# Hybrid streaming encoder step: the sample stage's loads all issued by the sync engine, the output weights split at that stage's tail, and the projection's last stores awaited inside it

## The chip, the core and the metric

The kernel runs on one core of a Trainium2 chip. The metric is the device time of one execution in microseconds (us); lower is better. The engines are PE (matrix products), DVE (vector), ACT (scalar activations), POOL and SP. SP computes nothing here, it issues DMAs. ACT can issue DMAs too, and while it does it computes nothing.

## What is computed

One layer of an encoder runs for one prompt (2048 tokens) and eight short sample streams (8 x 16 tokens = one tile of 128 rows), which share all weights:

```python
h = _rmsnorm(x, g_mix) * (1 + sc1) + sh1
qa, ka, va, qb, kb, vb, ob, ib, fb, zc, xbc, dtc, ud, vd = _split_cols(h @ w_in, IN_SIZES)
y_a = _band_attention(qa, ka, va, k_hist, v_hist, a_rel_bias)      # samples: 512 cached keys each
hb, new_bc, new_bn, new_bm = _mlstm(qb, kb, vb, igate, logf, b_c, b_n, b_m)
yc, new_ssm = _ssd(xs, dt, a, bm, cm, c_ssm)
mix = jnp.concatenate([y_a, y_b, y_c, y_d], axis=-1) @ w_out
x = x + gt1 * mix
x = x + gt2 * ((silu(causal_dwconv3(h2 @ w_gate)) * (h2 @ w_up)) @ w_down)
```

## The kernel before

Five stages follow each other, each a block in which every engine has its own written-out instruction order: `modulation` (0 to about 127 us of the profiled execution), `projections` (to about 834), `sample_stage` (to about 967), `mixers` (to about 1527), `feed_forward` (to the end). Between two stages all engines meet at a barrier (`Semaphores.give_back`, which also clears the stage's semaphores). No engine starts a stage before SP has passed the last waits of the stage before.

- **End of `projections`.** SP issues the last stores: the convolution rows to the scratch tensor `xc`, then `p_c_conv`, three DMAs of 768 single 4-byte elements each (L437). Then it waits for every store of the stage (L440 to L447), and the barrier follows.
- **`sample_stage`.** SP issues the loads of the cached keys and values (`k_in`, `v_in`, 8 + 8 DMAs of 512 KB) and of the SSM states (`ssm`, 8 of 128 KB). ACT, ahead of its first activation, issues everything else: gate parameters (`row_par`, `m0`), `qt`, `tok`, `xc`, `qa`, `k_new`, `v_new`, eight bias pieces, the mLSTM states `cst` (4 DMAs of 64-element rows and 4 of single elements, `state_b_n`), `gc` and `skip` (L1496 to L1518). PE then turns keys, computes scores for two streams at a time, multiplies with the old states (`old_c`, L1371, which waits for all of `cst`; `old_h`), and so on to `new_h` (L1427). DVE first places `qa` in `q_blk` (L1707), then builds the gate rows (L1710 to L1742). At the end SP stores `y`, the attention rows `ya` and the new states, `s_c_ssm` last (L1298).
- **`mixers`.** It multiplies with `w_out` in a split form: `w_hi` is the weight rounded to the PE's fast format (ACT, L2329), `w_lo` the remainder (DVE, L2590), and each product is three matmuls (L2148 to L2150). The eight slices of `w_out` are loaded through two buffers at the head of this stage; slice n+2 is loaded once `w_lo` of slice n is made. ACT's order is: slices 0 and 1, `decays(0)` (L2325), slices 2 to 7, and then the loop over the tiles, whose first step keeps `xs_b` (L2340). DVE's order is: wait for `params` (band, `gc`, four `skip_col` loads), two memsets of `band`, `skip`, `add_columns(0)` (L2454), the eight `w_lo`, then the loop. PE begins with `turn_xs` (L2053), which waits for `skip`. The first loop step multiplies the sample tile with `w_out`.

The two orders on ACT and DVE in `mixers`:

```python
for n in range(KD):                                   # ACT, L2327
    act.wait_ge(s_w[n % 2], 16 * (n // 2 + 1))
    a.activation(w_hi[:, KO[n], :], w_raw[n % 2], ACT.Copy).then_inc(E["w_hi"], 1)
    if n == 1:
        decays(0)
for n in range(KD):                                   # DVE, L2588
    dve.wait_ge(E["w_hi"], n + 1)
    v.tensor_tensor(w_lo[:, KO[n], :], w_raw[n % 2], w_hi[:, KO[n], :], ALU.subtract).then_inc(E["w_lo"], 1)
```

Of the kernel before, what the change touches and what calls it, by code (L numbers as in the profile page):

```python
# [11 lines left out]
P = 128  # L12
# [213 lines left out]
def projections(nc, sem, A, O, S, c, keep, par, w_hi, w_lo):  # L226
# [17 lines left out]
    with ExitStack() as ctx:  # L244
# [87 lines left out]
        def _(sp):  # L332
# [108 lines left out]
            for n in range(2):  # L441
                sp.wait_ge(s_xst[n], 16 * sum(len(tokens(m // KX)) for m in range(KX * NGR) if m % 2 == n))
# [4 lines left out]
            sp.wait_ge(s_copy, 16 * N_COPIES)  # L447
# [186 lines left out]
        def _(dve):  # L634
# [381 lines left out]

C_FLOOR, C_WB, C_WC, C_A, C_NCS = range(5)


def modulation(nc, sem, A, S, c, const_program, keep, par, w_hi, w_lo):  # L1020

    with ExitStack() as ctx:
# [25 lines left out]
        s_gout, s_par = sem("gates_stored"), sem("params_loaded")  # L1048
# [34 lines left out]
        def _(act):  # L1083
# [13 lines left out]
            act.wait_ge(s_par, 16 * len(par["loads"](A)))  # L1097

# [101 lines left out]
def sample_stage(nc, sem, A, O, S, c, par):  # L1200
# [4 lines left out]
    with ExitStack() as ctx:  # L1205
        sb, ps = new_pools(nc, ctx, "s_")
        W1 = DH + 1
        k_in, v_in = sb("k_in", [P, NB, NPAST, GW]), sb("v_in", [P, NB, NPAST, GW])
        k_t = sb("k_t", [P, 2, NB, HIST])
# [9 lines left out]
        row_par = sb("row_par", [H, 6])  # L1219
        cst, m0 = sb("cst", [P, 2, NB, W1]), sb("m0", [H, NB])  # L1220
# [19 lines left out]
        gc, skip = sb("gc", [P, GW]), sb("skip", [P, H])  # L1240
# [7 lines left out]
        names = """rows_loaded att_in bias_loaded mix_in par_in cst_loaded ssm_loaded  # L1248
# [15 lines left out]
        def _(sp):  # L1264
# [6 lines left out]
            for j in range(NG):  # L1271
                load_kv(2 * j)
                load_kv(2 * j + 1)
                if j == 0:
                    for b in range(NB):
                        sp.dma_start(ssm[half(b), b // 2], A["state_c_ssm"][0, b].rearrange("h p n -> p h n")
                                     ).then_inc(E["ssm_loaded"], 16)
                load_v(2 * j)
                load_v(2 * j + 1)
            sp.wait_ge(E["ready"], 1)  # L1280
# [212 lines left out]
        def _(act):  # L1493
            a = nc.scalar
            step = Steps(act, E["act"])
            for n, name in enumerate(("b_i_bias", "b_f_bias", "c_dt_bias", "c_a_log")):  # L1496
                act.dma_start(row_par[:, n:n + 1], A[name].rearrange("a h -> h a"), allow_slow_non_contiguous=True
                              ).then_inc(E["rows_loaded"], 16)
            act.dma_start(m0[:], A["state_b_m"][0].rearrange("b h -> h b"), allow_slow_non_contiguous=True
                          ).then_inc(E["rows_loaded"], 16)  # L1500
            act.dma_start(qt[:], S["qb"][:, :, SEQ:SEQ + P]).then_inc(E["mix_in"], 16)
            act.dma_start(tok[:], S["tok"][SEQ:SEQ + P, :]).then_inc(E["mix_in"], 16)
            act.dma_start(xc[:], S["xc"][:, :, SEQ:SEQ + P]).then_inc(E["mix_in"], 16)
            act.dma_start(qa[:], S["qa"][:, :, SEQ:SEQ + P]).then_inc(E["att_in"], 16)
# [32 lines left out]
            act.wait_ge(E["rows_loaded"], 80)  # L1537
# [47 lines left out]
            keep_probs(3)  # L1585

        @block.gpsimd
        def _(pool):
# [11 lines left out]
            pool.wait_ge(E["par_in"], 32)  # L1600
# [52 lines left out]
        def _(dve):  # L1653
# [183 lines left out]
            extract(3)  # L1837
            for h in range(H):
                add_h(h)


def mixers(nc, sem, A, O, S, c, keep, par):

# [5 lines left out]
    with ExitStack() as ctx:  # L1849
# [61 lines left out]
        def _(sp):  # L1911
# [82 lines left out]
            for n in range(2, KD):  # L1994
                load_w(n)
# [1301 lines left out]
```

## Time and profile before

| | |
|---|---|
| median of 3 runs | 3177.63 us (3173.46 to 3180.89) |
| the profiled execution | 3168.1 us, of which the span of instructions is 3166.4 us |
| PE busy in the span | 2846.8 us (90%) |
| DVE, ACT, POOL busy | 1297.1, 982.1, 245.0 us |
| HBM traffic | 285.75 MB read, 70.10 MB written |

The profiled execution is 9.5 us shorter than the median. Its span differs from its own time by 1.7 us. "Busy" is the time in which an engine executes an instruction; issuing a DMA is not counted as busy, although the engine can do nothing else meanwhile.

### The profile page before, as it was taken

What the parts mean: (1) busy time and instruction counts of PE and PEld (TensorE: products, weight loads), DVE (VectorE), ACT (ScalarE), POOL (GpSimd) and SP (SyncE); (2) the same over time, 40 slices, a digit from 0 to 9 for tenths busy, and PEclk for the clock granted to TensorE, in tenths of its full rate; (3) what the DMA queues carried; (4) which work ended last, traced back from release to release, by engine and by line L of the source; (5) the groups of instructions that cost most, each with busy time, mean ns of one, the idle gap of its engine ahead of it and who ended that gap; (6) DMA issues with size and microseconds to landing.
All of it is one profiled execution on the core that took longest, in us unless ns stands there. A gap on an engine that the chain in (4) does not pass through costs nothing.

```text
span 3166.4 us, 41936 instructions
## 1 busy us (share of the span) xinstructions
PE 2846.8 (90%) x16292; PEld 2548.5 (80%) x16292; DVE 1297.1 (41%) x2483; ACT 982.1 (31%) x1682; POOL 245.0 (8%) x413
## 2 busy tenths in 40 slices
PE   4499999999272999999599999999999999999987
PEld 1288888999252788887599998789999878999975
DVE  2333334342142554554233334544433454544444
ACT  1133334332131444444222223332222333222333
POOL 0000000000021432332000000000000000000000
PEclk8699999999685999999699999999999999999998
DMA  9622324211517444342522224433222443322344
GB/s 296 213 72 93 109 71 153 89 67 70 166 15 201 152 140 126 125 129 71 138 61 66 60 66 141 158 109 104 64 62 66 135 156 113 114 73 74 99 130 145
DMA packets 342266, 355.48 MB, mean 112 GB/s; under 512 B 44423, under 2 KB 283659, under 8 KB 341684
## 3 DMA queue, kind: packets, MB, share of 16 engines
q1 hardware_dynamic: 326738, 349.02, 35.4%
q10 hardware_dynamic: 15396, 4.66, 0.8%
q8 instruction: 88, 1.44, 0.2%
q14 instruction: 44, 0.36, 0.0%
HBM read 285.75 MB, written 70.10 MB: 112 GB/s over the span
## 4 chain that ended last, share of the span: by engine, by line
PE 46%; DVE 2%; DMA 2%; SPq 1%; issue 1%; ACT 0%; POOL 0%; DVEq 0%; ACTq 0%
PE acc_ps L2873 14%; PE acc_ps L2829 11%; PE acc_ps L2830 11%; PE acc_ps L2831 11%; DMA w_raw<-in_f_w_down 1%; DMA xr<-scratch_x 0%; DVE y L3121 0%; SPq L2773 0%; DVE w_lo L3095 0%; DMA out_y_prompt<-y 0%; ACT w_hi L2968 0%; DVE xr L3115 0%; DMA ffn_gate_in<-scratch_ffn_gate 0%; DVE prod L3109 0%; DVE w_lo L3038 0%
## 5 line engine op out<-in xcount | busy, mean ns | idle before, releaser
L2829 PE MATMUL acc_ps<-h_hi,w_hi 128*128 128x384 f32 (+1 forms) x2112 | 690.3, 327 | 6.3 <-DVE w_lo L3038 6.1
L2830 PE MATMUL acc_ps<-h_lo,w_hi 128*128 128x384 f32 (+1 forms) x2112 | 689.5, 326 | 0.0
L2831 PE MATMUL acc_ps<-h_hi,w_lo 128*128 128x384 f32 (+1 forms) x2112 | 689.5, 326 | 0.0
L3038 DVE TENSOR_TENSOR w_lo<-w_raw,w_hi 128x1024 fp32r<-128x1024 f32 x242 | 296.5, 1225 | 662.7 <-ACT w_hi L2926 652.9
L2926 ACT ACTIVATE w_hi<-w_raw 128x1024 fp32r<-128x1024 f32 x242 | 256.6, 1060 | 800.5 <-PE acc_ps L2831 524.0
L2829 PEld LDWEIGHTS acc_ps<-h_hi,w_hi 128*128 128x128 f32 x2112 | 397.9, 188 | 7.8 <-DVE w_lo L3038 6.5
L2830 PEld LDWEIGHTS acc_ps<-h_lo,w_hi 128*128 128x128 f32 x2112 | 397.9, 188 | 0.1
L2831 PEld LDWEIGHTS acc_ps<-h_hi,w_lo 128*128 128x128 f32 x2112 | 397.8, 188 | 0.0
L2873 PE MATMUL acc_ps<-w_hi,mid_hi 128*128 128x512 f32 x748 | 236.1, 397 | 30.3 <-DVE mid_lo L3099 15.8
L2873 PE MATMUL acc_ps<-w_hi,mid_lo 128*128 128x512 f32 x748 | 233.2, 393 | 0.0
L2873 PE MATMUL acc_ps<-w_lo,mid_hi 128*128 128x512 f32 x748 | 233.0, 393 | 0.0
L881 PE MATMUL p_unit<-w_in_hi,p_ht_hi 128*128 128x512 f32 (+1 forms) x544 | 203.2, 373 | 2.1 <-ACT p_m L490 2.1
L881 PE MATMUL p_unit<-w_in_hi,p_ht_lo 128*128 128x512 f32 (+1 forms) x544 | 200.9, 369 | 0.0
L881 PE MATMUL p_unit<-w_in_lo,p_ht_hi 128*128 128x512 f32 (+1 forms) x544 | 200.3, 368 | 0.0
L2873 PEld LDWEIGHTS acc_ps<-w_hi,mid_hi 128*128 128x128 f32 x748 | 139.5, 190 | 69.5 <-DVE mid_lo L3099 22.4
L940 PE MATMUL p_unit<-p_ht_hi,w_in_hi 128*128 128x384 f32 (+1 forms) x576 | 190.2, 330 | 2.8 <-DVE p_ht_lo L707 1.6
L941 PE MATMUL p_unit<-p_ht_lo,w_in_hi 128*128 128x384 f32 (+1 forms) x576 | 189.2, 329 | 0.0
L942 PE MATMUL p_unit<-p_ht_hi,w_in_lo 128*128 128x384 f32 (+1 forms) x576 | 188.6, 327 | 0.0
L2873 PEld LDWEIGHTS acc_ps<-w_lo,mid_hi 128*128 128x128 f32 x748 | 142.0, 190 | 30.3
L2873 PEld LDWEIGHTS acc_ps<-w_hi,mid_lo 128*128 128x128 f32 x748 | 142.0, 190 | 30.1
L3024 POOL TENSOR_SCALAR ff_mean<-ff_ss 128x1 f32<-128x1 f32 x17 | 8.7, 510 | 1629.1 <-ACT prod L2973 1629.1
L3073 DVE TENSOR_TENSOR mid<-gate_on,acc_ps 128x384 f32 (+3 forms) x132 | 64.3, 529 | 162.6 <-PE acc_ps L2831 162.6
(490 smaller groups left out, 4155.7 us busy)
## 6 DMA issues: line engine op xcount, KB each, us to landing
w_raw<-in_f_w_down SPq DMA_DIRECT2D x122, 512.0 KB, 3.5
w_raw<-in_f_w_gate SPq DMA_DIRECT2D x66, 512.0 KB, 3.9
w_raw<-in_f_w_up SPq DMA_DIRECT2D x66, 512.0 KB, 3.9
w_ada<-in_w_ada SPq DMA_DIRECT2D x12, 2048.0 KB
m_bc<-scratch_bc SPq DMA_DIRECT2D x16, 768.0 KB, 5.1
scratch_tok<-p_m SPq DMA_DIRECT2D x17, 640.0 KB, 2.9
m_tok<-scratch_tok SPq DMA_DIRECT2D x16, 640.0 KB, 4.8
scratch_ht<-p_m SPq DMA_DIRECT2D x17, 512.0 KB, 3.3
```

What stands on the lines that cost most here:

```text
L881: last = t.matmul(dst, a[j][:, k, :], b[:, k, at:at + w], start=(k == 0 and a is th_hi and b is w_hi), stop=(k == KD - 1 and a is th_lo))
L940: t.matmul(dst, w_hi[:, k, cols], hi, start=(k == 0), stop=False)
L941: t.matmul(dst, w_hi[:, k, cols], lo, start=False, stop=False)
L942: last = t.matmul(dst, w_lo[:, k, cols], hi, start=False, stop=(k == KD - 1))
L2829: t.matmul(dst, hi, h2_hi[:, k, cols], start=(k == 0), stop=False)
L2830: t.matmul(dst, hi, h2_lo[:, k, cols], start=False, stop=False)
L2831: last = t.matmul(dst, lo, h2_hi[:, k, cols], start=False, stop=(k == KD - 1))
L2873: last = t.matmul(acc[:, pair, half, :], lhs[j][:, cols], rhs[j][:, half * 512:(half + 1) * 512], start=begin, stop=(stop and lhs is m_lo))
L2926: a_.activation(w_hi[j][:], raw[j][:], ACT.Copy).then_inc(s_hi[j], 1)
L3024: nc.gpsimd.tensor_scalar(mean[:, j:j + 1], ss[:, j:j + 1], 1.0 / D, EPS, ALU.mult, ALU.add).then_inc(s_mean, 1)
L3038: v.tensor_tensor(w_lo[j][:], raw[j][:], w_hi[j][:], ALU.subtract).then_inc(s_lo[j], 1)
L3073: last = v.tensor_tensor(at_f(mid, f)[:, at:at + w], gate_on[:, at:at + w], u_ps[:, b, 0:w], ALU.mult)
```

## The change

- **Projection's last waits.** SP no longer waits at the end of `projections` for the `xc` stores and for five copies (`p_c_conv` among them). Their three semaphores survive the barrier, and the waits (`p_stored`) stand in `sample_stage`: on POOL before it writes `v1`, on DVE before `nums`, on SP before the store of `y`.
- **Parameters.** `row_par`, `m0`, `gc`, `skip` and `skip_col` become persistent (`par[...]`) and are loaded in `modulation` by 11 DMAs from ACT, behind the bias rows. The loads of the same data in `sample_stage` (7) and `mixers` (5) are gone.
- **Sample loads.** ACT issues none. SP issues all: `tok`, `xc`, `qt`, keys 0 and 1, `qa`, `k_new`, `v_new`, bias, `ssm`, values 0 and 1, `cst`, and then the other keys and values.
- **Output weights.** Once all keys are turned, SP loads the eight slices of `w_out` into the keys' buffer (now called `w_raw`). Behind the last attention copy ACT makes `w_hi` (in the memory of the turned keys), behind the last state DVE makes `w_lo` (in place of `w_raw`). `mixers` loads and splits nothing; there `skip` and `add_columns(0)` stand ahead of the wait for `band`.
- In `projections`, `m_row` and `diag` become views of the tile `vn`.

```diff
@@ projections, SP
-            for n in range(2):
-                sp.wait_ge(s_xst[n], 16 * sum(len(tokens(m // KX)) for m in range(KX * NGR) if m % 2 == n))
-            sp.wait_ge(s_copy, 16 * N_COPIES)
+        def stored(engine):
+            for n in range(2):
+                engine.wait_ge(s_xst[n], 16 * sum(len(tokens(m // KX)) for m in range(KX * NGR) if m % 2 == n))
+            engine.wait_ge(s_copy, 16 * N_COPIES)
@@ modulation, ACT
             rel_store(act)
+            for dst, at in par["more"](A):
+                act.dma_start(dst, at, allow_slow_non_contiguous=True).then_inc(s_more, 16)
@@ sample_stage, SP
-            for j in range(NG):
+            sp.dma_start(tok[:], S["tok"][SEQ:SEQ + P, :]).then_inc(E["mix_in"], 16)
+            sp.dma_start(xc[:], S["xc"][:, :, SEQ:SEQ + P]).then_inc(E["mix_in"], 16)
+            sp.dma_start(qt[:], S["qb"][:, :, SEQ:SEQ + P]).then_inc(E["mix_in"], 16)
+            load_kv(0)
+            load_kv(1)
...
+            for j in range(1, NG):
                 load_kv(2 * j)
                 load_kv(2 * j + 1)
...
                 load_v(2 * j)
                 load_v(2 * j + 1)
+            sp.wait_ge(E["k_turned"], 2 * NB)
+            w_view = A["w_out"][0].rearrange("(k p) n -> k p n", p=P)
+            for k in range(KD):
+                sp.dma_start(w_raw[:, k, :], w_view[k]).then_inc(E["w_loaded"], 16)
+            p_stored(sp)
@@ sample_stage, ACT
-            for n, name in enumerate(("b_i_bias", "b_f_bias", "c_dt_bias", "c_a_log")):
-                act.dma_start(row_par[:, n:n + 1], A[name].rearrange("a h -> h a"), allow_slow_non_contiguous=True
-                              ).then_inc(E["rows_loaded"], 16)
...
-            act.dma_start(skip[:], A["c_d_skip"][0].partition_broadcast(P)).then_inc(E["par_in"], 16)
...
             keep_probs(3)
+            act.wait_ge(E["w_loaded"], 16 * KD)
+            act.wait_ge(E["scores"], NG)
+            for k in range(KD):
+                a.activation(w_hi[:, k, :], w_raw[:, k, :], ACT.Copy).then_inc(E["w_high"], 1)
@@ sample_stage, POOL
+            pool.wait_ge(E["mix_in"], 48)
+            p_stored(pool)
             step(g.memset(v1[:, :, DH:W1], 1.0))
-            pool.wait_ge(E["mix_in"], 48)
@@ sample_stage, DVE
             dve.wait_ge(E["qc_kept"], 1)
+            p_stored(dve)
             step(v.tensor_tensor(nums[:], qc[:], spread(col[:, R_INTER, :], 2, W1), ALU.mult))
...
+            for k in range(KD):
+                dve.wait_ge(E["w_high"], k + 1)
+                v.tensor_tensor(w_lo[:, k, :], w_raw[:, k, :], w_hi[:, k, :], ALU.subtract).then_inc(E["w_low"], 1)
@@ mixers, ACT
-            for n in range(KD):
-                act.wait_ge(s_w[n % 2], 16 * (n // 2 + 1))
-                a.activation(w_hi[:, KO[n], :], w_raw[n % 2], ACT.Copy).then_inc(E["w_hi"], 1)
-                if n == 1:
-                    decays(0)
+            decays(0)
@@ mixers, DVE
-            dve.wait_ge(E["params"], 16 * N_PARAMS)
...
             for g in range(2):
                 v.tensor_scalar(skip[:, g, :], c["ident"][:], skip_col[:, g:g + 1], None, ALU.mult).then_inc(E["skip_made"], 1)
             add_columns(0)
-            for n in range(KD):
-                dve.wait_ge(E["w_hi"], n + 1)
-                v.tensor_tensor(w_lo[:, KO[n], :], w_raw[n % 2], w_hi[:, KO[n], :], ALU.subtract).then_inc(E["w_lo"], 1)
+            dve.wait_ge(E["band_loaded"], 16)
@@ the kernel
-                projections(nc, sem, A, O, S, c, keep, par, w_hi, w_lo)
+                p_stored = projections(nc, sem, A, O, S, c, keep, par, w_hi, w_lo)
+            sem.give_back(but=("p_xc_stored0", "p_xc_stored1", "p_copies"))
```

On ACT, at the start of the sample stage, this stood before (the last of its loads and its first activations; `s_` is the stage's prefix of tile names, `s_m` the PSUM tile):

```order
L1510 DMA s_bias_in<-scratch_rel 16x528 x8
L1513 DMA s_cst<-in_state_b_c 64x8x64
L1515 DMA s_cst<-in_state_b_n 64x8x1
L1513 DMA s_cst<-in_state_b_c 64x8x64
L1515 DMA s_cst<-in_state_b_n 64x8x1
L1513 DMA s_cst<-in_state_b_c 64x8x64
L1515 DMA s_cst<-in_state_b_n 64x8x1
L1513 DMA s_cst<-in_state_b_c 64x8x64
L1515 DMA s_cst<-in_state_b_n 64x8x1
L1517 DMA s_gc<-in_c_norm_g 128x256
L1518 DMA s_skip<-in_c_d_skip 128x4
L1538 ACT_TABLE_LOAD
```

Of these rows only the table load is still on ACT; it is the first thing that ACT does in the stage. The loads of `s_cst` now stand on SP. There, in the changed kernel, the order from the stage's start to the first two of them is this (`sample_k` is the keys' buffer):

```order
L1280 DMA s_tok<-scratch_tok 128x1280
L1281 DMA s_xc<-scratch_xc 128x6x128
L1282 DMA s_qt<-scratch_qb 128x2x128
L1275 DMA sample_k<-in_cache_a_k 128x1024 x2
L1285 DMA s_qa<-scratch_qa 128x2x128
L1286 DMA s_k_new<-scratch_ka 128x2x128
L1287 DMA s_v_new<-scratch_v 16x8x256
L1291 DMA s_bias_in<-scratch_rel 16x528 x8
L1294 DMA s_ssm<-in_state_c_ssm 64x4x128 x8
L1278 DMA s_v_in<-in_cache_a_v 128x1024 x2
L1299 DMA s_cst<-in_state_b_c 64x8x64
L1301 DMA s_cst<-in_state_b_n 64x8x1
```

What was spread over two issuing engines is now one sequence: 26 loads stand ahead of the eight of `cst`, and the other twelve of keys and values behind them. On DVE, from the sample stage's last states to the mixers' first column sums, before:

```order
L1693 TENSOR_TENSOR s_ssm<-s_m,s_ssm 128x4x128 x4
L1205 UNCONDITIONAL_BRANCH
L2441 UNCONDITIONAL_BRANCH
L2574 TENSOR_SCALAR m_mask<-tri 128x128
L2575 MEMSET m_cst 128x130
L2576 MEMSET m_hst 128x256
L2578 SCALAR_TENSOR_TENSOR par_col<-par_col 128x64
L2580 COPY m_dec_c<-par_dec 64x32 x2
L2583 MEMSET m_band 64x4x64
L2584 MEMSET m_band 64x4x64
L2586 TENSOR_SCALAR m_skip<-ident,m_skip_col 128x128 x2
L2454 TENSOR_TENSOR m_bc<-m_bc,par_col 128x1024
```

and now:

```order
L1853 TENSOR_TENSOR w_out_lo<-sample_k,w_out_hi 128x1024 x8
L2562 TENSOR_SCALAR m_mask<-tri 128x128
L2563 MEMSET m_cst 128x130
L2564 MEMSET m_hst 128x256
L2566 SCALAR_TENSOR_TENSOR par_col<-par_col 128x64
L2568 COPY m_dec_c<-par_dec 64x32 x2
L2571 TENSOR_SCALAR m_skip<-ident,par_skip_col 128x128 x2
L2442 TENSOR_TENSOR m_bc<-m_bc,par_col 128x1024
L2574 MEMSET m_band 64x4x64
L2575 MEMSET m_band 64x4x64
```

The eight remainders of the weights moved from behind `m_bc` to ahead of the stage's barrier, and the memsets of `band` moved behind `m_skip` and `m_bc`.

## Rows read from the trace of the kernel before

**Rows 1.** Windows by stage: busy us of each engine, PE clock, DMA share, GB/s.

```profile
834.00:873.00 39.00, 2.33 (x9) 1.35 (x9) 1.90 (x8) 0.04 (x1) 1.33 (x4) 0.50 1.05 303
...
967.00:1010.00 43.00, 4.60 (x20) 3.65 (x21) 12.22 (x18) 10.27 (x11) 5.94 (x7) 0.50 0.73 253
```

**Rows 2.** SP at the projection's end: its timeline (start, us), then its waits.

```profile
815.35 1.71 SPq L437 DMA_DIRECT2D out_p_c_conv<-p_m  x3
...
SPq L447 <- DMA out_p_c_conv<-p_m: 15.1, 1, 15.1
```

**Rows 3.** ACT's timeline in the sample stage, its first 40 us.

```profile
835.65 0.63 ACTq L1501 DMA_DIRECT2D s_qt<-scratch_qb  x1
...
843.93 0.69 ACTq L1513 DMA_DIRECT2D s_cst<-in_state_b_c  x1
...
845.34 6.05 ACTq L1513 DMA_DIRECT2D s_cst<-in_state_b_c  x1
...
871.81 0.64 ACTq L1517 DMA_DIRECT2D s_gc<-in_c_norm_g  x1
...
872.96 1.28 ACT L1538 ACT_TABLE_LOAD   x1 [58.00 <-issue]
```

**Rows 4.** PE's timeline in the sample stage.

```profile
834.00 0.80 PE L1432 MATMUL s_m<-ident,par_gates_s 128*4 128x128 f32 x3 [22.64 <-PEq L3254]
...
887.17 3.30 PE L1371 MATMUL s_m<-s_qt,s_cst 64*65 64x16 f32 x64 [0.78 <-ACT s_hst L1557]
...
923.28 1.06 PE L1313 MATMUL s_m<-ident,s_k_in 128*128 128x128 f32 x8 [1.27 <-ACT s_k_t L1523]
```

**Rows 5.** DVE's timeline in the sample stage.

```profile
852.75 0.98 DVE L1707 COPY s_q_blk<-s_qa 64x128 f32<-64x128 f32 x4 [11.30 <-DMA s_v_new<-scratch_v]
876.97 0.14 DVE L1710 TENSOR_SCALAR s_row_par<-s_row_par 4x1 f32<-4x1 f32 x1 [23.25 <-ACT s_soft L1544]
...
882.85 0.14 DVE L1742 TENSOR_SCALAR s_row_par<-s_row_par 4x1 f32<-4x1 f32 x1
```

**Rows 6.** Windows while small stores are under way, and at full rate; columns as in rows 1.

```profile
819.00:832.00 13.00, 0.00 (x0) 0.00 (x0) 0.00 (x0) 0.00 (x0) 0.00 (x0) 0.50 0.00 0
861.00:863.00 2.00, 0.00 (x0) 0.00 (x0) 0.00 (x0) 0.00 (x0) 0.00 (x0) 0.50 1.06 392
1521.00:1526.00 5.00, 0.00 (x0) 0.00 (x0) 0.00 (x0) 0.00 (x0) 0.00 (x0) 0.50 0.00 0
```

**Rows 7.** SP's timeline at the sample stage's end.

```profile
949.78 11.20 SPq L1298 DMA_DIRECT2D out_s_c_ssm<-s_ssm  x7
```

**Rows 8.** DMA issues around the mixers' end: KB each, us from issue to landing.

```profile
out_p_c_ssm<-m_prod SPq DMA_DIRECT2D x1, 128.0 KB, 7.8
```

**Rows 9.** The mixers' head: timelines of SP, POOL, DVE, ACT and PE.

```profile
966.72 0.57 SPq L1928 DMA_DIRECT2D m_xc<-scratch_xc  x1
...
974.03 0.44 SPq L1986 DMA_DIRECT2D m_y<-scratch_y_s  x1
...
978.00 1.41 POOL L2394 TENSOR_TENSOR m_bc<-m_bc,m_xc 128x256 f32<-128x256 f32 x2
...
986.47 0.27 DVE L2583 MEMSET m_band<- 64x256 f32 x1 [18.71 <-DMA m_skip_col<-in_c_d_skip]
...
1008.95 0.58 ACT L2340 ACTIVATE m_xs_b<-m_m_ps 128x512 f32<-128x512 f32 x1
...
1012.69 0.79 PE L2148 MATMUL m_m_ps<-m_w_hi,m_yt_hi 128*128 128x512 f32 x1
```

**Rows 10.** DMA issues in the mixers' head, columns as in rows 8.

```profile
m_y<-scratch_y_s SPq DMA_DIRECT2D x1, 384.0 KB, 9.9
```

**Rows 11.** ACT's timeline in the modulation.

```profile
52.82 1.71 ACT L218 ACTIVATE w_in_hi<-w_tok_raw 128x1804 fp32r<-128x1804 f32 x1 [31.59 <-DMA w_tok_raw<-in_w_in]
```

**Rows 12.** The page's costliest groups, two of them (mean ns of one behind busy us).

```profile
L3038 DVE TENSOR_TENSOR w_lo<-w_raw,w_hi 128x1024 fp32r<-128x1024 f32 x242 | 296.5, 1225 | 662.7 <-ACT w_hi L2926 652.9
L2926 ACT ACTIVATE w_hi<-w_raw 128x1024 fp32r<-128x1024 f32 x242 | 256.6, 1060 | 800.5 <-PE acc_ps L2831 524.0
```

More of the change, by code:

```diff
@@ L1097, in _ @@
             act.wait_ge(s_par, 16 * len(par["loads"](A)))
+            act.wait_ge(s_more, 16 * len(par["more"](A)))
         @block.vector
@@ L1197, with sample_stage @@
 R_INTER, R_FLOOR, R_WB, R_CS, R_WC, R_A, R_NCS, R_DT = range(ROWS)
-def sample_stage(nc, sem, A, O, S, c, par):
+def sample_stage(nc, sem, A, O, S, c, par, w_raw, k_turned, w_hi, w_lo, p_stored):
     NG = NB // 2
@@ L1218, in sample_stage @@
         tok, qt, xc = sb("tok", [P, T_W]), sb("qt", [P, 2, P]), sb("xc", [P, KX, P])
-        row_par = sb("row_par", [H, 6])
-        cst, m0 = sb("cst", [P, 2, NB, W1]), sb("m0", [H, NB])
+        row_par, m0, gc, skip = par["row"], par["m0"], par["gc"], par["skip"]
+        cst = sb("cst", [P, 2, NB, W1])
         ssm, hst = sb("ssm", [P, NG, H, P]), sb("hst", [P, NG, H, P])
@@ L1839, in _, with mixers @@
                 add_h(h)
-def mixers(nc, sem, A, O, S, c, keep, par):
+            for k in range(KD):
+                dve.wait_ge(E["w_high"], k + 1)
+                v.tensor_tensor(w_lo[:, k, :], w_raw[:, k, :], w_hi[:, k, :], ALU.subtract).then_inc(E["w_low"], 1)
+def mixers(nc, sem, A, O, S, c, keep, par, w_hi, w_lo):
     NM = NT + 1
@@ L1850, in mixers @@
         sb, ps = new_pools(nc, ctx, "m_")
-        w_hi, w_lo = sb("w_hi", [P, KD, D], F32R), sb("w_lo", [P, KD, D], F32R)
-        gc, skip = sb("gc", [P, GW]), sb("skip", [P, 2, P])
-        skip_col = sb("skip_col", [P, 2])
+        gc, skip_col, skip = par["gc"], par["skip_col"], sb("skip", [P, 2, P])
         gate = sb("gate", [P, D])
@@ L2139, in out_part @@
                     k = KO[q]
-                    if mm == 0 and hf == 0:
-                        pe.wait_ge(E["w_lo"], q + 1)
                     if hf == 0 and q in (0, 4):
@@ L3199, in params @@
         "gd": [P, GW], "gb": [P, GW], "gate_bias": [P, 3 * H], "na": [P, H], "taps": [P, 5, KX],
+        "row": [H, 6], "m0": [H, NB], "gc": [P, GW], "skip": [P, H], "skip_col": [P, 2],
         "gates": [P, 3 * H, NT], "gates_s": [P, 3 * H], "dt": [P, H, NT], "col": [P, 5, H * NT], "dec": [P, 2, H * NT]}.items()}
@@ L3210, in loads, with more @@
         return out
-    par["loads"] = loads
+    def more(A):
+        out = [(par["row"][:, n:n + 1], A[name].rearrange("a h -> h a"))
+               for n, name in enumerate(("b_i_bias", "b_f_bias", "c_dt_bias", "c_a_log"))]
+        out += [(par["m0"][:], A["state_b_m"][0].rearrange("b h -> h b")), (par["gc"][:], A["c_norm_g"][0].partition_broadcast(P)),
+                (par["skip"][:], A["c_d_skip"][0].partition_broadcast(P))]
+        out += [(par["skip_col"][h % 2 * DH:h % 2 * DH + DH, h // 2:h // 2 + 1], A["c_d_skip"][0, h:h + 1].partition_broadcast(DH))
+                for h in range(H)]
+        return out
+    par["loads"], par["more"] = loads, more
     return par
@@ L3249, in __init__, with give_back @@
         self.nc, self.made, self.group = nc, {}, []
-    def give_back(self):
-        self.nc.clear_and_free_semaphores(self.group)
+    def give_back(self, but=()):
+        kept = [self.made[name] for name in but]
+        self.nc.clear_and_free_semaphores([s for s in self.group if not any(s is k for k in kept)])
         self.nc.all_engine_barrier()
-        self.group = []
+        self.group = kept
     def __call__(self, name):
```

96 lines of the change are left out of this document (38 added, 58 removed).

## Prediction

> **What bounds the kernel now.** The windows by stage come first, because the page's 90% PE is an average over stages with different limits. In the sample stage's first 39 us PE is busy 2.3 us, and in the mixers' first 43 us 4.6 us [rows 1]. The change touches only these stretches and the gap ahead of them. PE waits in three places, which I read in order of time.
>
> First gap: SP has issued the last `p_c_conv` store at 817.1 and waits 15.1 us for its landing; only then comes the barrier [rows 2]. PE starts the sample stage at 834.0 [rows 4].
>
> Second gap: ACT spends 834 to 872.5 on issuing loads. Single issues take up to 6.05 us, against 0.63 us for the early ones, and the first table load comes at 872.96, with "issue" as what held it [rows 3]. DVE's gate rows (876.97) wait for ACT's softplus [rows 5], PE for ACT's copies. The DMA engines are full in that stretch (share 1.05, 303 GB/s) [rows 1], and the last loads are ACT's of 871.8 [rows 3], so the traffic ends at about 873. So two limits end at nearly the same time, and a change that frees only ACT must still be measured against the transfers. From 887.17, the product with the old mLSTM states [rows 4], there is no wait for a load until the end; the mixers start at 966.72 [rows 9], 79.5 us later. The last 17 us of this are stores; SP issues seven of them from 949.78 on and needs 11.2 us for it, 1.6 us each [rows 7].
>
> Third gap: in the mixers DVE stands until 986.5 for `skip_col`, which PE's first work needs, and then PE waits for ACT's `xs_b`, which stands behind the eight `w_hi` until 1008.95. The first product with the output weights starts at 1012.69, 46.0 us after the stage's start [rows 9].
>
> **The projection's waits.** 15.1 us leave the barrier [rows 2]; the sample stage starts at 834.0 - 15.1 = 818.9. The other stores awaited there were issued earlier and had landed by then (SP names only this one). POOL meets `p_stored` ahead of `v1`, DVE ahead of `nums`, more than 20 us behind the old states, SP ahead of `y`. All are later than 832.3, so the moved wait costs nothing on DVE and SP; on POOL `v1` is wanted much later still. Without that cover it would cost up to 832.3 - 818.9 = 13.4 us.
>
> But are loads issued at 818.9 held by the 2304 small stores under way? They stand in the trace until 832.3, but from 819 to 832 the DMA engines are empty [rows 6]. At the mixers' end a 128 KB store behind other small stores had moved its last data by 1521 [rows 6] and was reported 7.8 us behind its issue [rows 8]. So data move past an unconfirmed store, but the report is late. I take it that the new loads' data flow from 819 on and their reports come at 832.3 at the earliest. The Trainium skill, "DMA: Bandwidth & Descriptors", section "Queues, rings and completion order", says that a semaphore increment lands only after every earlier write from that DMA engine, across its queues; the trace agrees, by the 7.8 us of a store whose data needed less than 3. Without this rule the reports of `tok` and `qa` could come from about 826 on, and the sum would be 1 to 2 us better; with it, it is the sum below.
>
> **The sample stage's start.** What is late next is the later of two routes to the old states' product.
> - *Compute route.* ACT's softplus needs no load any more (parameters are resident) and is over within 6 us of the start. DVE places `qa` (0.98 us) from 832.4 on, then the gate rows take 882.99 - 876.97 = 6.0 us, and from there to the product it was 887.17 - 882.99 = 4.2 us [rows 4, 5]. 832.4 + 1.0 + 6.0 + 4.2 = 843.6.
> - *Load route.* `cst` stands behind 26 loads on SP. By issue time: 18 of the loads ahead at 0.63 us, the eight of `ssm` and the eight of `cst`, which are cut as finely, at 0.69 us [rows 3], make 11.3 + 11.0 = 22 us. By traffic: the whole took 873 - 834 = 39 us; the twelve 512 KB loads now behind `cst` are 6.3 MB, at 392 GB/s [rows 6] 16 us, which leaves 23 us. 818.9 + 23 = 841.9, and some 2 us more until the report. The upper bound is ACT's own issue of these eight loads, 871.81 - 843.93 = 27.9 us with full rings [rows 3]: 818.9 + (22.3 - 5.5) + 27.9 = 863.6.
>
> I take 846, near the lower end, because the row of 27.9 us shared its time with SP's 6 MB of keys and values, which now stand behind. Bounds: 841 and 863.6. The product starts 887.2 - 846 = 41 us earlier (24 to 46); this contains the 15.1.
>
> Keys 2 and 3 are wanted 7.7 us later, at 854; they stand right behind `cst` and need 3 us. The last of them is there by 818.9 + 39 + 2 = 860, and PE turned the last keys 36 us behind the product [rows 4]. So the remaining 79.5 us stay as they are: no engine there got shorter.
>
> **The sample stage's tail.** SP issues 4.2 MB of weights when the last keys are turned (924.3 before, 883 now) and behind them waits with `y`, `ya`, the states. At 392 GB/s they take 11 us. The state stores come 25 us behind them (949.8 - 924.3), the smaller stores of `y` and `ya` in between, so nothing that ends the stage is held [rows 4, 6, 7]. ACT's eight `w_hi` and DVE's eight `w_lo` (a tile of 128x1024 takes 1060 and 1225 ns [rows 12], so 8.5 and 9.8 us) lie beside the 17 us of stores. If that cover were gone they would cost 10 us. I take 0 (0 to 3).
>
> **The mixers' head.** Gone: the waits for `skip_col`, eight loads, eight `w_hi`, eight `w_lo`. What is late next is POOL's `bc`, ready at 978.0 + 1.4 = 979.4 [rows 9], which does not move against the stage's start. DVE adds the columns (1.2 us) and ACT takes the exponential (1.1 us), both over 128x1024 elements as in [rows 12], and `xs_b` starts at 981.9; the sample's `y` lands, with 1 MB of weights no longer ahead of it (2.7 us), at 974.03 + 9.9 - 2.7 = 981.2 [rows 9, 10]. From `xs_b` to the first product it was 1012.69 - 1008.95 = 3.7 us. 981.9 + 3.7 = 985.6, I take 986.7: 20 us instead of 46 behind the start, a gain of 26 us. Bounds: 18 us if all that DVE did before 1008 must still follow `y`, and 28.
>
> **Modulation.** Eleven more small loads, at some 0.5 us each, are issued by ACT in an idle time of 31.6 us [rows 11]; 0.13 MB cost the full DMA engines 0.3 us and some packets. I take 1 us lost (0 to 2).
>
> **The sum.** 41 + 26 - 1 = 66 us. Against the profiled execution: 3168.1 - 66 = 3102. The runs' median is 9.5 us above it, so the prediction is 3177.6 - 66 = 3112 us.
>
> **Rivals.**
> - *The loads are held until 832.3* (13%). The small stores occupy the rings and nothing moves meanwhile. For: in the sample's own tail, behind the small stores of `s_b_n`, an issue of SP takes 1.6 us instead of 0.63 [rows 3, 7]. Against: the store at the mixers' end, whose data were out by 1521 [rows 6]. Then `cst` lands at 832.3 + 23.4 = 856 and the sum is 31 + 26 - 1 = 56: 3121 us.
> - *`cst` is bound by its issue* (12%). The eight DMAs of 256-byte and 4-byte pieces take on SP what they took on ACT: product at 863, sum 24 + 26 - 1 = 49: 3129 us.
> - *ACT's issuing was only the visible part* (7%). Work starts when all traffic is over, as before (873 + 14 = 887): 818.9 + 39 + 14 = 872, sum 15 + 26 - 1 = 40: 3138 us. The Trainium skill's same page, section "Issuing engines are not separate DMA queues", speaks for this: issuing from several engines saves only issue time, "usually small relative to the DMA itself". The row against it is ACT's 58 us with "issue" as releaser [rows 3].
> - *Slower* (4%). One mechanism: SP's ring of descriptors stays full, and each of the 24 small loads costs SP an issue like ACT's worst (6.05 us) instead of 0.5 to 0.7; that is 145 us before keys 2 to 7 are issued. It decides from a mean of 4.3 us: then SP issues keys 2 at 922, the mixers start at 998, the 31 us lost eat the 26 gained, and with 1 us from the modulation we are 6 us up: 3184 us. ACT's eight had a mean of 3.5 us, but beside a second full queue.
> - *No effect* (2%): two of the above in part, 3177 us.
> - *More than I sum* (4%): reports are not held and `y` comes earlier, 46 + 28 - 0 = 74: 3104 us or a little less.
>
> The forecast's own case has 58%.
>
> **How the numbers follow.** 3112 is the likeliest case. Low end: the most of each term, 3104, less some 6 us because three runs spread by 3.7 us to either side: 3098. High end: it takes in the rivals at 3121 and 3129 with their spread and ends at 3134. Outside are the all-traffic case, slower, no effect and part of "more": about 15%. One measurement cannot tell less than 0.2% (6 us) from no change. All cases but the last two named as such lie further down: faster 0.94, same 0.02, slower 0.04.
>
> **What the changed profile would show.** The first sample work on PE at 819, not 834; no table load held by issue; reports of `tok` and `qa` at 832 or just behind; the product with the old states at 846 (842 to 850) with `cst` or the gate rows as releaser; 79 us from there to the mixers' first DMA; eight `w_hi` and `w_lo` over before SP's last wait; `skip` on DVE within 2 us of the mixers' start, and the first output product 20 us behind it. Wrong would be: weights in the sample tail that push the last store, a product behind 855, or a mixers' head that still waits for a load behind 985 - 967 = 18 us.

## The result and the profile after

The changed kernel takes 3129.95 us (median, 3119.36 to 3133.14); the kernel before, run beside it, 3179.26 us. The ratio is 0.984, 95% interval 0.9812 to 0.9869: 49 us less, where 66 were forecast. The profiled execution took 3130.6 us (span 3128.8).

Where the profiled pair stands at six marks (us from the span's start; those of before are in [rows 4, 9], save the first, which is PE's first projection product, and the last, SP's first DMA of the FFN, which are read from the same timelines):

| mark | before | after | moved |
|---|---|---|---|
| first product of the projection | 148.9 | 149.7 | +0.8 |
| PE starts the sample stage | 834.0 | 819.5 | -14.5 |
| product with the old mLSTM states | 887.2 | 860.5 | -26.7 |
| mixers' first DMA | 966.7 | 944.4 | -22.3 |
| first product with the output weights | 1012.7 | 964.2 | -48.5 |
| first DMA of the FFN | 1527.8 | 1485.9 | -41.9 |

The stage starts 15 us earlier, as forecast, but its loads are slow. SP's timeline (start, us; the answer to [rows 3], whose loads SP issues now):

```profile
815.69 1.70 SPq L438 DMA_DIRECT2D out_p_c_conv<-p_m  x3
819.45 0.34 SPq L1280 DMA_DIRECT2D s_tok<-scratch_tok  x1
819.84 2.54 SPq L1281 DMA_DIRECT2D s_xc<-scratch_xc  x1
822.43 5.35 SPq L1282 DMA_DIRECT2D s_qt<-scratch_qb  x1
...
834.14 4.48 SPq L1287 DMA_DIRECT2D s_v_new<-scratch_v  x1
838.66 3.72 SPq L1291 DMA_DIRECT2D s_bias_in<-scratch_rel  x8
842.43 5.59 SPq L1294 DMA_DIRECT2D s_ssm<-in_state_c_ssm  x8
...
857.14 0.64 SPq L1301 DMA_DIRECT2D s_cst<-in_state_b_n  x1
```

SP stands 5.35 us at `qt`, the third load of the stage. What the DMA engines moved meanwhile is in the windows (columns as in [rows 1]; the last is GB/s):

```profile
819.00:823.00 4.00, 0.80 (x3) 0.24 (x3) 1.02 (x4) 3.22 (x5) 0.52 (x1) 0.50 0.00 0
823.00:827.00 4.00, 0.00 (x0) 0.00 (x0) 0.00 (x0) 0.79 (x2) 0.00 (x0) 0.50 0.60 37
827.00:831.00 4.00, 0.00 (x0) 0.00 (x0) 0.00 (x0) 0.00 (x0) 0.00 (x0) 0.50 1.15 51
831.00:835.00 4.00, 0.00 (x0) 0.00 (x0) 0.00 (x0) 0.00 (x0) 0.00 (x0) 0.50 0.69 28
835.00:839.00 4.00, 0.00 (x0) 0.00 (x0) 0.00 (x0) 0.00 (x0) 0.00 (x0) 0.50 0.63 126
839.00:843.00 4.00, 1.91 (x9) 1.89 (x10) 0.00 (x0) 0.72 (x2) 0.86 (x3) 0.50 1.07 380
```

Nothing moves until 823, then 28 to 51 GB/s although the engines' packets fill the time (share up to 1.15), and full rate comes only at 839. The three stores of `p_c_conv`, issued 815.7 to 817.4, land later than in the kernel before, too (the landing row of `out_p_c_conv`, before and then after):

```profile
DMA to landing us min/median/max: 8.4/10.2/15.9
DMA to landing us min/median/max: 11.0/11.3/19.6
```

If the longest is the last issued (at 816.8; before, 816.5 + 15.9 is the end of SP's wait), it ends at about 836, just ahead of the full rate. PE waits for the loads three times:

```profile
841.09 0.69 PE L1469 MATMUL s_m<-ident,s_tok 128*128 128x128 f32 x2 [20.81 <-DMA s_qt<-scratch_qb]
...
852.80 1.83 PE L1395 MATMUL s_m<-ident,s_ssm 128*128 128x128 f32 x8 [3.61 <-DMA s_ssm<-in_state_c_ssm]
...
860.50 5.98 PE L1404 MATMUL s_m<-s_qt,s_cst 64*65 64x16 f32 x64 [3.82 <-DMA s_cst<-in_state_b_n]
```

ACT on the other hand is free at once: its first table load starts at 819.45, against 872.96 in [rows 3]. The tail and the mixers' head, in SP's, ACT's and DVE's, then PE's timelines (the answers to [rows 7, 9]):

```profile
920.39 0.65 SPq L1325 DMA_DIRECT2D out_s_b_n<-s_cst  x1
...
925.87 15.21 SPq L1331 DMA_DIRECT2D out_s_c_ssm<-s_ssm  x8
944.41 0.57 SPq L1937 DMA_DIRECT2D m_xc<-scratch_xc  x1
...
915.48 7.67 ACT L1597 ACTIVATE w_out_hi<-sample_k 128x1024 fp32r<-128x1024 f32 x8
960.17 0.58 ACT L2328 ACTIVATE m_xs_b<-m_m_ps 128x512 f32<-128x512 f32 x1
...
923.29 9.16 DVE L1853 TENSOR_TENSOR w_out_lo<-sample_k,w_out_hi 128x1024 fp32r<-128x1024 f32 x8
945.49 0.48 DVE L2571 TENSOR_SCALAR m_skip<-ident,par_skip_col 128x128 f32<-128x128 f32 x2
957.45 1.73 DVE L2442 TENSOR_TENSOR m_bc<-m_bc,par_col 128x1024 f32<-128x1024 f32 x1 [11.47 <-POOL m_bc L2380]
...
964.18 0.79 PE L2140 MATMUL m_m_ps<-w_out_hi,m_yt_hi 128*128 128x512 f32 x1
```

`w_hi` and `w_lo` lie beside the stage's last stores, DVE begins `skip` 1.1 us behind the mixers' start, and the first output product comes 19.8 us behind it (46.0 before).

By this mark the pair has gained 48.5 us, and the medians differ by 49. The profiled pair itself differs by 37.6: in the profiled run of after, the mixers took 521.7 us from that product to the FFN (515.1 before), with TensorE at a lower clock in two stretches, 30 to 50 us behind that product, where before had 1.00:

```profile
994.20:1004.20 10.00, 8.35 (x46) 7.41 (x46) 8.01 (x19) 1.48 (x5) 4.21 (x3) 0.78 0.49 164
1004.20:1014.20 10.00, 10.00 (x50) 8.60 (x50) 1.92 (x6) 0.78 (x3) 1.96 (x5) 0.71 0.44 146
```

Among the eight kernels below, which have the same mixers behind their head, this distance is 513 to 522 us, so most of it varies with the run. The FFN, which the change doesn't touch, takes another 4 us more in that run, and the profiled run of before was 11 us faster than the median beside it. I therefore read the change from the marks up to 964.

### The profile page after: what moved, and what is told of

The parts are those of the page before. It is cut to its first block, busy times and chain, and to the rows that moved or that the text cites. A ratio compares the mean times of both kernels' runs of the same rounds, so it can differ in the third digit from the quotient of the medians.

```text
span 3128.8 us, 41943 instructions
## 1 busy us (share of the span) xinstructions
PE 2858.1 (91%) x16292; PEld 2559.3 (82%) x16292; DVE 1297.4 (41%) x2483; ACT 982.2 (31%) x1682; POOL 245.2 (8%) x413
## 4 chain that ended last, share of the span: by engine, by line
PE 48%; DMA 2%; DVE 1%; SPq 1%; issue 1%; ACT 0%; POOL 0%; DVEq 0%
PE acc_ps L2858 14%; PE acc_ps L2816 11%; PE acc_ps L2814 11%; PE acc_ps L2815 11%; DMA w_raw<-in_f_w_down 1%; DMA xr<-scratch_x 0%; DVE y L3106 0%; SPq L2758 0%; DMA out_y_prompt<-y 0%; DVE xr L3100 0%; DMA ffn_gate_in<-scratch_ffn_gate 0%; DVE prod L3094 0%; DVE w_lo L3023 0%; DVE w_lo L3080 0%; DVE mid L3124 0%
```

## Experiments

Two theories. **A:** the 2304 four-byte stores of `p_c_conv` hold the loads issued behind them, so the wait taken off SP turns up again in the DMA engines. **B:** the stores play no part; the loads are slow by their own issue and their own small pieces. Each kernel is timed as a ratio to the kernel before, run in the same session. Marks are from each one's profile.

| kernel | ratio (95% interval) | median, us | sample stage's first DMA | old states' product | mixers start | output product |
|---|---|---|---|---|---|---|
| before | 1 | 3179.3 | 834.0 | 887.2 | 966.7 | 1012.7 |
| changed | 0.984 (0.9812 to 0.9869) | 3130.0 | 819.5 | 860.5 | 944.4 | 964.2 |
| e1 conv late | 0.9794 (0.9767 to 0.9821) | 3116.2 | 820.8 | 847.1 | 939.1 | 957.7 |
| e2 wait back | 0.9833 (0.9807 to 0.9858) | 3127.5 | 838.9 | 865.0 | 949.9 | 969.0 |
| e3 loads on ACT | 0.9899 (0.9871 to 0.9928) | 3151.3 | 822.4 | 889.1 | 973.0 | 992.0 |
| e4 head only | 0.9915 (0.9886 to 0.9943) | 3154.3 | 837.2 | 887.3 | 971.4 | 991.0 |
| e5 b_n rows | 0.9811 (0.9790 to 0.9832) | 3113.2 | 821.3 | 860.5 | 933.9 | 952.6 |
| e6 skip back | 0.9857 (0.9832 to 0.9881) | 3128.9 | 821.1 | 860.7 | 943.8 | 969.0 |
| e7 lo in mixers | one run | 3126.1 | 821.8 | 861.3 | 945.8 | 965.3 |
| e8 both rows | 0.9766 (0.9746 to 0.9786) | 3100.8 | 819.6 | 845.1 | 920.0 | 938.6 |

The median of before was 3180.6 beside e1 to e4 and 3173.2 beside e5 to e8, so differences between the sessions are taken from the ratios.

### e1: the small stores behind the loads

```diff
-            for n in range(3):
-                sp.dma_start(O["p_c_conv"][0, 0, n].rearrange("(k p) -> p k", p=P), xbuf[:, :, TW + n],
-                             allow_slow_non_contiguous=True).then_inc(s_copy, 16)
+            sp.wait_ge(s_conv_kept, 1)
...
+            v.tensor_copy(par["conv"][:], xbuf[:, :, TW:TW + 3]).then_inc(s_conv_kept, 1)
...
             p_stored(sp)
+            for n in range(3):
+                sp.dma_start(O["p_c_conv"][0, 0, n].rearrange("(k p) -> p k", p=P), par["conv"][:, :, n],
+                             allow_slow_non_contiguous=True).then_inc(E["stored"], 16)
             sp.wait_ge(E["ready"], 1)
```

> The changed kernel, but the three p_c_conv stores (2304 elements of 4 bytes) leave the projection: DVE copies the 128x18 elements into a resident tile, and SP issues the stores in the sample stage, behind the eight loads of the output weights. Nothing is left out. Theory A (the small stores hold the sample's loads): the DMA engines move data at once from 818 on instead of trickling until 838, the product with the old states moves from 860.5 to 843 to 848, and the kernel takes 12 to 18 us less than the changed one: 3112 to 3118 us. Theory B (the loads are slow by their own issue and their own small pieces; the stores play no part): product at 858 to 861, time within 3 us of 3130. If the stores in their new place push the stage's last store, up to 15 us of the gain comes back as a later start of the mixers.

Two windows of e1, then its SP timeline:

```profile
819.00:823.00 4.00, 0.80 (x3) 0.24 (x3) 1.02 (x4) 1.92 (x4) 0.52 (x1) 0.50 0.40 125
823.00:827.00 4.00, 0.00 (x0) 0.00 (x0) 0.00 (x0) 2.09 (x3) 0.00 (x0) 0.50 1.00 337
```

```profile
821.71 0.64 SPq L1282 DMA_DIRECT2D s_qt<-scratch_qb  x1
...
891.57 6.76 SPq L1314 DMA_DIRECT2D out_p_c_conv<-par_conv  x3
898.37 2.87 SPq L1317 DMA_DIRECT2D scratch_y_s<-s_y  x1
...
901.66 12.87 SPq L1324 DMA_DIRECT2D scratch_y_s<-s_ya  x8
```

The same load `qt` is issued in 0.64 us, data flow at 337 GB/s where 37 were, and the product stands at 847.1. Theory A holds and B falls: no load of the sample stage had changed, only what was ahead of it. But the stores hold in their new place too: SP issues `ya` in 12.9 us instead of 8.7, and from the product to the mixers it is 92.0 us instead of 83.9. Of 13.4 us gained at the product 8 are given back. By the ratios e1 is 0.46% (14.6 us) ahead of the changed kernel, more than the 6.5 us at the output product (8.8 if counted from the projection's first product, which came 2.4 us later here). The intervals overlap a little, so the ratios leave the size open; the marks give 6.5 to 8.8 us.

### e2: the projection's wait put back

```diff
             sp.wait_ge(s_gst, 16 * (4 * H + 1))
+            for n in range(2):
+                sp.wait_ge(s_xst[n], 16 * sum(len(tokens(m // KX)) for m in range(KX * NGR) if m % 2 == n))
+            sp.wait_ge(s_copy, 16 * N_COPIES)
```

> The changed kernel with the projection's last stores awaited on SP inside the projection again, as before the change; all else as changed. Theory A (the loads were held by the stores anyway): the sample stage starts at 834.5 instead of 819.5, its loads then flow at once, and the product with the old states comes 25 to 27 us behind the start, at 860 to 862: no loss, 3130 to 3133 us. Theory B (data flow past the unconfirmed stores, as the prediction assumed, and the product is late by issue alone): everything moves by the 15 us of the wait, product at 875, 3145 us.

SP waits for `p_c_conv` again (SP's waits: us in total, times, longest) and the stage starts at 838.9:

```profile
SPq L448 <- DMA out_p_c_conv<-p_m: 16.8, 1, 16.8
```

That start is 4 us later than expected: the stores were issued 2.4 us later than in the changed kernel (818.06 and 815.69), and the wait was 16.8 us and not 15.1. But the stage's first loads are there 6.9 us behind the start instead of 21.6 (PE's timeline):

```profile
845.79 0.69 PE L1472 MATMUL s_m<-ident,s_tok 128*128 128x128 f32 x2 [6.04 <-DMA s_qt<-scratch_qb]
...
864.95 5.97 PE L1407 MATMUL s_m<-s_qt,s_cst 64*65 64x16 f32 x64 [2.81 <-DMA s_cst<-in_state_b_n]
```

The distance from the issue of `p_c_conv` to the product is 46.9 us here (864.95 - 818.06) and 44.8 us in the changed kernel (860.50 - 815.69). The moved wait is thus worth 2 us of its 15 (16.8 here), and the times can't be told apart (0.9833 and 0.984). That the product stands at 865.0 and not at the expected 860 to 862 is the later start.

### e3 and e4: the sample's loads on ACT, with the wait moved and not

```diff
-            sp.dma_start(tok[:], S["tok"][SEQ:SEQ + P, :]).then_inc(E["mix_in"], 16)
...
         def _(act):
+            act.dma_start(qt[:], S["qb"][:, :, SEQ:SEQ + P]).then_inc(E["mix_in"], 16)
+            act.dma_start(tok[:], S["tok"][SEQ:SEQ + P, :]).then_inc(E["mix_in"], 16)
...
```

e4 has e2's waits besides. So it is the kernel before with resident parameters and the output weights split in the sample's tail.

> The changed kernel with tok, qt, xc, qa, k_new, v_new, the eight bias rows and the eight of cst issued by ACT again, in the order of before; the parameters stay resident, the waits stay moved, the output weights stay in the sample stage. Theory A (ACT's issuing delayed its own first activation, and that was most of the 39 us of before): ACT's table load comes 36 to 39 us behind the stage's start or, held by the small stores, 10 us later still; product with the old states 13 to 14 us behind it, at 869 to 882 instead of 860.5; 3138 to 3152 us. Theory B (all traffic bounds the start, whoever issues): product within 3 us of 860.5, 3130 us.

> The kernel before with one part of the change: the output weights loaded and split in the sample stage's tail, parameters resident; the sample's loads are on ACT and the waits inside the projection, as before. By the prediction's term for the mixers' head, 26 us, plus some 3 us for the five parameter loads that ACT no longer issues in the sample stage, less 0.3 for the modulation: 3150 us (3146 to 3156). Rival: the two parts are not additive, because the weights' loads in the tail cost the stores more where the sample stage is later: then 3158 or more.

ACT's timeline of e3:

```profile
822.43 0.61 ACTq L1513 DMA_DIRECT2D s_qt<-scratch_qb  x1
...
832.08 8.92 ACTq L1517 DMA_DIRECT2D s_k_new<-scratch_ka  x1
...
850.41 8.02 ACTq L1527 DMA_DIRECT2D s_cst<-in_state_b_n  x1
...
874.15 1.28 ACT L1546 ACT_TABLE_LOAD   x1 [55.89 <-issue]
```

The price of ACT's issuing is e4 against e2: the product is 50.2 us behind the stage's start instead of 26.0, and the ratios 0.9915 and 0.9833 are 26 us apart. The traffic is the same in both, so "all traffic must end first" falls. e3 against e4 is the second proof for A: it starts 15 us earlier and has its product 2 us later. PE's first loads come 27.6 us behind the start in e3 and 10.9 us in e4, although the small stores went through SP's queue and these loads through ACT's. So it is not SP's queue alone that holds them; the DMA engines, or what lies behind them, are left, and no run tells these two apart. e3's time was as expected, its product came 7 us behind the latest that was expected, because ACT's issuing lasted until 51.7 us behind the start (46 to 49 expected).

e4 alone gives 27 us by its ratio, and its output product is 19.6 us behind the mixers' start: the prediction's 26 us for the head. By the mark of that product it is 21.7 us ahead of before, because its tail takes 84.1 us instead of 79.5. Of these 1.7 us are the product with the old states (PE's timeline of e4):

```profile
887.33 5.01 PE L1391 MATMUL s_m<-s_qt,s_cst 64*65 64x16 f32 x64 [0.78 <-ACT s_hst L1568]
```

### e5: one of the tail's small stores as rows

```diff
-                sp.dma_start(O["s_b_n"][0, :, h].rearrange("b d -> d b"), cst[half(h), h // 2, :, DH],
-                             allow_slow_non_contiguous=True).then_inc(E["stored"], 16)
+            sp.dma_start(O["s_b_n"][0].rearrange("b h d -> b (h d)"), n_rows[:]).then_inc(E["stored"], 16)
...
+            for a in range(2):
+                last = t.transpose(m[0:NB, B_E, a * P:(a + 1) * P], cst[:, a, :, DH], ident[:])
+            last.then_inc(E["n_turned"], 1)
...
+            v.tensor_copy(n_rows[:], m[0:NB, B_E, 0:GW]).then_inc(E["n_kept"], 1)
```

> The changed kernel with one store written differently: the four s_b_n stores (2048 elements of 4 bytes), issued in the sample's tail ahead of the eight s_c_ssm stores, become one store of eight rows of 1 KB, after two PE transposes and a DVE copy. Theory A (small stores hold whatever is issued behind them): the eight s_c_ssm issues take 5 to 6 us instead of 15.2, the mixers start 8 to 10 us earlier, and the time is 3120 to 3123 us. Theory B (the s_c_ssm stores are slow by their own pieces): their issue stays at 15 us and the time at 3130.

SP's timeline of e5:

```profile
920.35 0.47 SPq L1325 DMA_DIRECT2D out_s_b_n<-s_n_rows  x1
...
923.63 5.31 SPq L1331 DMA_DIRECT2D out_s_c_ssm<-s_ssm  x8
933.91 0.57 SPq L1944 DMA_DIRECT2D m_xc<-scratch_xc  x1
```

The eight `s_c_ssm` stores are the same as before and are issued in 5.31 us instead of 15.21; the mixers start 10.5 us earlier. By the ratios it is 9 us, in intervals that overlap (the median is lower than expected because that of before is, too). It is theory A again, at a second place.

### e6 and e7: parts of the mixers' head

e6 loads `gc` and `skip_col` in the mixers again and lets DVE wait for them ahead of `skip`. e7 makes `w_lo` on DVE at the mixers' start instead of in the sample's tail.

```diff
+            for h in range(H):
+                sp.dma_start(skip_col[h % 2 * DH:h % 2 * DH + DH, h // 2:h // 2 + 1],
+                             A["c_d_skip"][0, h:h + 1].partition_broadcast(DH)).then_inc(E["params"], 16)
...
+            dve.wait_ge(E["params"], 80)
```

```diff
+            for k in range(KD):
+                v.tensor_tensor(w_lo[:, k, :], w_raw[:, k, :], w_hi[:, k, :], ALU.subtract)
```

> The changed kernel, but gc and skip_col are loaded in the mixers again, in their old place behind band, and DVE waits for them ahead of skip as before; the output weights stay split in the sample stage. Prediction's reading: of the 26 us of the head the wait for skip_col is the smaller part. skip_col lands some 17 us behind the stage's start (19.7 before, less 1 MB of weights), then 1.2 + 1.1 + 3.7 us to the first product: 23 to 24 us behind the start instead of 19.8, 3 to 4 us lost, 3134 us. Rival: the wait for skip_col alone carried most of the head: product 30 us or more behind the start, 3140 or more.

> The changed kernel with DVE's eight w_lo (9.2 us) moved from the sample's tail, where they run beside the s_c_ssm stores, to the mixers' start ahead of skip. If DVE's subtraction slows those stores (12.05 us for the eight issues before the change, 15.2 after it, 16.6 in the two runs with ACT's loads), they return to 12 us; otherwise they stay at 15 to 16.6. The head of the mixers gets longer by what of the 9.2 us is not covered by POOL's bc: first output product 20 to 25 us behind the stage's start.

DVE's timeline of e6:

```profile
962.45 0.48 DVE L2576 TENSOR_SCALAR m_skip<-ident,par_skip_col 128x128 f32<-128x128 f32 x2 [17.61 <-DMA par_skip_col<-in_c_d_skip]
962.85 1.22 DVE L2446 TENSOR_TENSOR m_bc<-m_bc,par_col 128x1024 f32<-128x1024 f32 x1
```

In e6 the output product is 25.2 us behind the start, so the wait for `skip_col` is worth 5.4 us in the trace (0.9857 against 0.984 is 5 us, within the uncertainty; 0.9857 of 3179 is the 3134 expected), a little more than my 3 to 4. The rest of the 26 us left with the weights' own work. Before, ACT idled 1.0 to 3.6 us ahead of each of the last six `w_hi` for the load of its slice, as in this row of the kernel before:

```profile
993.43 1.06 ACT L2329 ACTIVATE m_w_hi<-m_prod 128x1024 fp32r<-128x1024 f32 x1 [3.56 <-DMA m_prod<-in_w_out]
```

No run has the eight `w_hi` back alone, so how the rest divides between them and their loads is read from such rows. In e7 the output product is 19.5 us behind the start: the 9.2 us on DVE fit into its wait for POOL's `bc`. The eight `s_c_ssm` issues took 14.4 us, no return to 12: in this one run, DVE's work beside them is not what made them slower.

### e8: no small stores ahead of anything

e5's row store, and `p_c_conv` the same way: DVE keeps 128x18 elements, PE transposes them at the sample stage's start, ACT copies, and SP stores 18 rows of 512 bytes behind the loads.

```diff
+            t.transpose(m[0:3 * KX, B_S, 0:P], par["conv"][:].rearrange("p n k -> p (n k)"), ident[:]).then_inc(E["conv_turned"], 1)
...
+            a.activation(conv_rows[:], m[0:3 * KX, B_S, 0:P], ACT.Copy).then_inc(E["conv_kept"], 1)
...
+            sp.wait_ge(E["conv_kept"], 1)
+            sp.dma_start(O["p_c_conv"][0, 0].rearrange("n (k p) -> (n k) p", p=P), conv_rows[:]).then_inc(E["stored"], 16)
```

> The candidate that should beat both kernels: the changed kernel with the one s_b_n store of eight rows as in e5, and p_c_conv kept in a resident tile, transposed by PE at the start of the sample stage, and stored by SP as one store of 18 rows of 512 bytes behind the sample's loads. By theory A: 14 us as in e1 for loads that flow at once, some 8 us more because no element stores stand in the tail (e1 lost these: 92 us from the old states' product to the mixers instead of 84), and 8 to 10 us as in e5: 3096 to 3102 us. By theory B 3116 or more.

PE's and SP's timelines of e8:

```profile
845.09 5.98 PE L1407 MATMUL s_m<-s_qt,s_cst 64*65 64x16 f32 x64 [2.77 <-DMA s_cst<-in_state_b_n]
...
909.74 5.31 SPq L1334 DMA_DIRECT2D out_s_c_ssm<-s_ssm  x8
920.03 0.57 SPq L1950 DMA_DIRECT2D m_xc<-scratch_xc  x1
```

It beats both kernels: 3100.8 us, ratio 0.9766 (0.9746 to 0.9786), 23 us by the ratios below the changed kernel, nearly half of what the whole change had brought. The product stands at 845, the output product 25.6 us ahead of the changed kernel's. The 3096 to 3102 us expected are met only because before was faster beside this run: 0.9766 of 3179 is 3105. The marks show 15.4 us at the product and 9.0 in the tail, 24.4 at the mixers' start. The expectation had taken e1's 14 us from its ratio, where e1's marks gave 6.5, and had added the 8 us of the tail to it.

## Why the prediction was right, and where it was not

The time fell in the range (3098 to 3134) and the sign was right, but 17 us of the forecast 66 did not come. Term by term:

- **Modulation, 1 us.** The projection's first product came 0.8 us later in the profiled pair, and 1.3 to 3.2 us later in the eight experiments, always against the one profile of before. The mean of the nine is 2.1, just beyond the bound of 2.
- **The wait leaves the barrier, 15.1 us.** The stage starts at 819.5 as forecast. POOL, DVE and SP met the moved wait without loss that the marks show. But the next step failed: "I take it that the new loads' data flow from 819 on". They did not. The rows that it rested on, a 128 KB store at the mixers' end with its last data out before 1521 [rows 6, 8], say nothing of loads behind 2304 elements of 4 bytes: the small stores ahead of that one were four of 64 elements, which landed within 5.2 us. The first rival's mechanism is what e1 and e2 show, and its row, the 1.6 us an issue behind `s_b_n` [rows 7], was the better witness; I gave it 13%. The window beside that row, in the kernel before, showed the same picture (columns as in [rows 1]): packets filled the engines' time, and 42 GB/s moved.

```profile
950.00:956.00 6.00, 0.00 (x0) 0.00 (x0) 0.00 (x0) 0.00 (x0) 0.00 (x0) 0.50 1.61 42
```

The rival's time was mis-sized too: full rate came at 839 and not at 832.3, and the stores themselves took longer: the slowest landed 18.0 to 20.1 us behind its issue in the five kernels with loads behind it, 15.9 to 17.9 in the three without (before, e2, e4). The stage's first loads took 21.6 us, which is the 15.1 us of the wait and the 6.6 us that they take without the stores (e1: 820.8 to 827.3).
- **ACT freed of issuing.** With the loads flowing, the product was forecast 27 us behind the stage's start; it is 26.0 in e2, 26.4 in e1 and 25.5 in e8, and e4 shows 50.2 with ACT's issuing. That is the 26 us that the term of 41 held beside the wait. The page "DMA: Bandwidth & Descriptors" of the Trainium skill, section "Issuing engines are not separate DMA queues", calls what issuing saves usually small; here the engine that issues is also wanted for work, and e4 against e2 measured 24 us at the product. The rivals "bound by issue" (product 863) and "all traffic first" are not needed: 860.5 is 819.5 + 15 + 26, and both mechanisms are shown apart.
- **The tail, 79.5 us, no loss.** It took 83.9. 2.7 us of these are the product with the old states itself, 5.98 us against 3.30 us [rows 4]. Windows of after:

```profile
856.00:860.00 4.00, 0.68 (x4) 0.41 (x2) 0.39 (x2) 1.91 (x4) 0.00 (x0) 0.93 0.81 106
860.50:863.00 2.50, 2.50 (x27) 2.50 (x27) 0.00 (x0) 0.00 (x0) 0.00 (x0) 0.50 1.02 406
```

PE is idle for most of 856 to 860, waiting for `cst`, and the product runs at a granted clock of 0.50 (the 1.2 GHz level); before, PE was busy without a pause of over 1 us from 877 on, and the product had 1.00. The idle time is not all of it: in e3 and e4 PE waited only 0.8 us ahead of the product and had 1.00 in the 4 us before it, as in the kernel before, yet the clock fell to 0.50 within the product, which took 4.83 and 5.01 us. Why it fell there and not in the kernel before stays open. The rest, 1.7 us, lies at the `s_c_ssm` stores: their eight issues take 14.4 to 16.7 us in the six changed kernels whose tail's stores are as they were, and 12.05 before. The cause stays open; e7, a single run, speaks against DVE's `w_lo`.
- **The mixers' head, 26 us.** 26.2 in the pair, and e4 shows it alone. The output product stood 19.8 us behind the start (20 forecast), and what came late next was POOL's `bc`, as the sum had it: it released DVE 13.0 us behind the start (12.7 forecast).

So 41 + 26 - 1 became 22.3 + 26.2 = 48.5 at the output product: 26.7 at the old states' product, with the projection's end shift inside it, less 4.4 in the tail. The step that failed is the 15.1 us, counted as a gain because SP stopped waiting. That the time still fell in the range comes from its upper end, which took in two rivals. The nearest time named, 3129 us for `cst` bound by its issue, is met by luck: that mechanism was not what made the product late, the loads held by the stores were (13 us of the sum), and the tail added 4.4.

## What to carry to other kernels

A wait for stores that is moved behind the start of the next stage need not be a gain: here the next stage wanted the DMA engines first, and 2 of 15 us were left. Look in the windows at what they do between the last store's issue and its landing, and where an almost empty stretch of 15 us stands behind element-wise stores, turn those into rows (a PE transpose and a copy) before moving the wait. The sign to look for is a cheap DMA that suddenly takes SP several us to issue; there were two such places here, worth 23 us together. Loads that have to queue go on an engine that only issues: on ACT, which also computes, they put the first dependent product 24 us later (e4 against e2).

## What the runs showed of the hardware

- Loads behind 2304 stores of 4 bytes moved nothing for 4 us and then 28 to 51 GB/s for 12 us, at a busy share of up to 1.15; the same loads without them moved 337 GB/s at a share of 1.00. Issued from ACT's queue, with the stores in SP's, the first loads were there 16.7 us later than without the stores (e3: 27.6 us, e4: 10.9); in SP's own queue it was 15.0 us (21.6 in the changed kernel, 6.6 in e1).
- The stores of 4 bytes were slower with loads behind them as well: the slowest of the three DMAs landed 15.9, 17.4 and 17.9 us behind its issue with nothing behind it (before, e4, e2) and 18.0 to 20.1 us with the loads (changed, e3, e5, e6, e7).
- The same eight `s_c_ssm` stores are issued in 5.31 us behind stores by rows (e5) and in 15.21 us behind 2048 stores of 4 bytes.
- A chain of 64 small matmuls takes 5.98 us at the lower clock level (granted clock 0.50) and 3.30 us at the higher (1.00); in e3 and e4 the clock fell within it, and it took 4.83 and 5.01 us.
